# Gathers of the value rows two places further ahead in GpSimd's order, in a hybrid decoder step with product-key experts

## What is computed

```python
act = jax.nn.gelu(jnp.einsum('thkd,td->thk', u_emb[idx], tb).astype(jnp.float32))
return jnp.einsum('thk,thkd->td', (g * act).astype(tb.dtype), v_emb[idx])
```

## Time and profile before

| | us |
|---|---|
| three runs | 2326.48, 2330.93, 2336.44; median 2330.93 |
| the profiled execution, its own time | 2352.97 |
| its span, first to last instruction | 2351.2 |
| busy in the span | TensorE matmul 1711.3 (73%), VectorE 1556.3 (66%), ScalarE 540.0 (23%), GpSimd 918.6 (39%) |
| DMA moved in the span | 798.79 MB, mean 340 GB/s |

### The profile page before, as it was taken

One profiled execution on the slowest core, in us unless ns is written; L12 is line 12 of the kernel. 1 busy time (PEld: TensorE's weight loads), 2 busy tenths in 40 slices (PEclk: granted clock), 3 DMA queues, 4 the chain that ended last, 5 costly groups with the idle time before them and its releaser, 6 DMA issues.

```text
span 2351.2 us, 30749 instructions
## 1 busy us (share of the span) xinstructions
PE 1711.3 (73%) x10511; PEld 1183.2 (50%) x10511; DVE 1556.3 (66%) x4092; ACT 540.0 (23%) x1574; POOL 918.6 (39%) x840
## 2 busy tenths in 40 slices
PE   7999977687898898987899879996534434343433
PEld 7899976443587776765577667663100000000000
DVE  4634178777578547888756776435388878877855
ACT  4446255100135123432122341111001000010000
POOL 0000001156434454543454455555644454444442
PEclk8999999757799999997899999997655566566566
DMA  6487767289999999986799899987999999999995
GB/s 226 148 269 251 249 198 266 81 307 405 398 398 381 402 409 359 359 312 215 275 379 349 337 388 388 401 336 289 397 421 422 421 417 421 417 415 413 414 421 234
DMA packets 181932, 798.79 MB, mean 340 GB/s; under 512 B 20977, under 2 KB 21233, under 8 KB 147857
## 3 DMA queue, kind: packets, MB, share of 16 engines
q0 software_dynamic: 119808, 570.48, 61.7%
q1 hardware_dynamic: 59616, 219.40, 25.6%
q10 hardware_dynamic: 2352, 6.95, 1.0%
HBM read 779.88 MB, written 12.14 MB: 337 GB/s over the span
## 4 chain that ended last, share of the span: by engine, by line
PE 20%; DMA 14%; DVE 11%; issue 5%; POOL 3%; ACT 0%; another core or an unknown queue 0%; POOLq 0%; DVEq 0%; ACTq 0%; SPq 0%
PE ps L490 11%; DMA s_exr<-in_uv,s_gidx 6%; DMA s_wr<-in_uv,s_gidx 3%; PE ps L817 3%; DVE s_exr L1722 2%; PE ps L800 2%; PE ps L473 2%; DMA s_scr<-in_uv,s_gidx 2%; DMA s_hnr<-in_uv,s_gidx 1%; DMA s_exr<-in_v,s_gidxT 1%; POOL s_exr L1379 1%; DVE s_wr L1722 1%; DVE s_scr L1722 1%; PE ps L839 0%; POOL s_exr L1365 0%
## 5 line engine op out<-in xcount | busy, mean ns | idle before, releaser
L490 PE MATMUL ps<-s_hnr,s_wr 128*128 128x256 f32 (+2 forms) x3968 | 679.9, 330 | 48.5 <-ACT s_hist_p L978 24.5
L490 PEld LDWEIGHTS ps<-s_hnr,s_wr 128*128 128x128 f32 x3968 | 610.3, 197 | 128.0 <-issue 73.8
L1334 POOL DMA_INDIRECT s_exr<-in_u,s_gidx x288 | 310.2, 1077 | 838.3 <-DVE s_act_z L1722 449.3
L1722 DVE CUSTOM_DVE_ANT_0 s_exr<-s_exr,s_tbg 128x1024 f32<-128x1024 f32 x407 | 491.7, 1221 | 167.1 <-DMA s_exr<-in_u,s_gidx 100.1
L1346 POOL DMA_INDIRECT s_exr<-in_v,s_gidxT x256 | 279.4, 1091 | 197.8 <-issue 89.8
L817 PE MATMUL ps<-s_exr,s_sw 128*32 128x512 f32 x476 | 156.5, 1044 | 164.0 <-DVE s_sw L1751 164.0
L1379 POOL DMA_INDIRECT s_exr<-in_uv,s_gidx x119 | 140.3, 1179 | 149.2 <-PE ps L817 120.9
L800 PE MATMUL ps<-s_exr,s_zb 128*32 128x512 f32 x1072 | 152.7, 659 | 41.6 <-DMA s_exr<-in_v,s_gidxT 29.6
L1427 DVE SCALAR_TENSOR_TENSOR s_scr<-s_scr,s_par 128x128 f32<-128x128 f32 (+2 forms) x288 | 122.2, 426 | 50.3 <-ACT s_scr L984 41.5
L817 PEld LDWEIGHTS ps<-s_exr,s_sw 128*32 128x32 f32 x476 | 25.0, 157 | 244.0 <-DVE s_sw L1751 191.6
L1157 ACT ACTIVATE s_gth<-s_g 128x4 f32<-128x4 f32 x64 | 13.1, 205 | 566.3 <-DVE s_g L1740 566.3
(11 more groups left out here) (314 smaller groups left out, 2695.6 us busy)
## 6 DMA issues: line engine op xcount, KB each, us to landing
s_wr<-in_wstream SPq DMA_DIRECT2D x360, 512.0 KB
s_tbg<-s_h2e ACTq DMA_DIRECT2D x36, 128.0 KB
s_exr<-in_u,s_gidx POOLq DMA_INDIRECT x288
s_exr<-in_v,s_gidxT POOLq DMA_INDIRECT x268
s_xr<-in_sample_h_in SPq DMA_DIRECT2D x8, 512.0 KB, 7.9
s_scr<-in_sample_h_in SPq DMA_DIRECT2D x8, 512.0 KB, 7.3
out_sample_h_out<-s_xr SPq DMA_DIRECT2D x8, 512.0 KB
out_sample_h_out<-s_scr SPq DMA_DIRECT2D x8, 512.0 KB
```

Of the source, the lines that this page charges most:

```text
L490: last = pe.matmul(ps[:, o % 2, 0:n], wring[:, slot, k, :], rhs[:, k, :], start=k == 0, stop=k == KT - 1)
L1334: pool.indirect_dma_start(uring[n % URING], None, a["u"], bass.IndirectOffsetOnAxis(ap=gidx[:, i % 2, s:s + 1], axis=0)).then_inc(u_in[n % ...
L1722: dve.tensor_tensor_reduce(out=u, in0=u, in1=tbg[:, i % 2, :], scale=1.0, scalar=0.0, op0=ALU.mult, op1=ALU.add, accum_out=act_z[:, i % 2, ...
```

## The change

Only the order in which GpSimd issues its gathers changes, for groups 0 to 7 of v with groups 1 to 8 of u. At the start of each pass two row sets of v are issued; from then on row set t + 2 of v stands ahead of u slot t, where row set t stood. The last two u slots of a pass follow each other with no v between them. No gather is added or removed, no buffer and no wait changes its form.

```diff
             for i in range(WIDE - 1):
+                gather_v(i, 0)
+                gather_v(i, 1)
                 for t in range(GT):
-                    gather_v(i, t)
+                    if t + 2 < GT:
+                        gather_v(i, t + 2)
                     gather_u(i + 1, t)
             for t in range(GT):
                 gather_old(WIDE - 1, t)
```

## The result

The changed kernel takes 2375.59 us in the median of five runs (2370.29 to 2378.06) against 2330.93 us of the kernel before, here also five runs: a ratio of 1.0185, 95% interval 1.0167 to 1.0203. The change makes the kernel slower by 44.7 us, where 17.5 us were forecast. The direction and the mechanism of the loss were right. The size was missed by a factor of 2.55, and the gain that the sum counted on did not come.

The account below looks back on a forecast made before the run. TensorE and the arrival of rows were taken to come near to setting the pace. Loss 33.5 us (15 + 3 + 4 + 9 + 2.5) less gain 16 made + 17.5 us: 2348 us, range given 2314 to 2376, the forecast's own 2343 to 2376.

Parts of the forecast that it names:

- the gain: TensorE's waits for v rows: 16 us saved, mainly 11.4 at the 1410 us stall and 3.5 near 1307; ends 0 and 22.
- The coupling (step 1): u slot 4k - 2, not 4k, stands behind the v gather waiting for TensorE's quad; VectorE gets two u slots later.
- The decode stage: 500 to 625 us: late u rows delay VectorE, then TensorE; three payments of 4.8 us, 15 us lost, ends 0 and 29.
- The bracket: Landing time of a gather, between 6.74 us for the quickest on the chain and 17.3 us in the decode stage's crowd.
- 785 to 910: DMA engines full, VectorE's next norm waits for the dots before it; two places at 2.1 us each, 3 us lost.
- 910 to 1150: 910 to 1040: 3 us, partly hidden behind TensorE; 1040 to 1150: late u slot 2 delays the dot before L612, 4 us.
- 625 to 785, 1150 to 1325: Same pattern of late u rows, half or more hidden behind TensorE's dense work; 2 us lost.
- The end of the alternation: Slots 26 and 27 stand behind the v gather of 1619.10, so the first `gather_old` goes late; 2.5 us, with longer landing 8.
- (B): Rival, a wash: lateness half hidden, or the 1410 stall's gain lost at the next DMA wait; 2332 us, chance 0.28.
- (A): Rival, relief wins: u's 4.8 us paid once inside VectorE's idle time, TensorE's stalls go; 2315 us, chance 0.17.
- (C): Rival: late dots delay TensorE, its quad v, v u, in every quad, landing as in the crowd; + 66, 2397 us, chance 0.08.

Follow-up runs that it names:

- pass 0 alone: Changed gather order in the first of the eight passes only (decode stage), other seven as in the kernel before; ratio 1.0071.
- the second profile: Later profile of the unchanged kernel before, made beside the experiments in a job of 2334 us; span 2330.1 us.
- pass12: Changed gather order in passes 1 and 2 only (623 to 920 us), the others as in the kernel before; ratio 1.0036.
- pass56: Changed gather order in passes 5 and 6 only (1227 to 1497 us), the others as in the kernel before; ratio 0.9983.

## Why the prediction was right in direction and wrong in size

**The coupling (step 1) is shown.** It rests on the run that kept the waiting gather's place, on TensorE's quads in two places under both orders, on the steps from one to three places, and on the traces: GpSimd's queue runs empty before each blocked v gather of the decode stage, and rows land no later than before. What failed is the size of three terms of the loss, and the gain, which is the largest error.

**The decode stage, 15 us forecast: 17 to 25.** The run of pass 0 alone costs 17 us, the trace of the whole change shows 24.7 in that stage by VectorE's first dots and 17.8 by TensorE's quads (from quad 0 to quad 0 of the next group, -2.8 to 15.0 us of difference). The prediction had one payment of 4.8 us if the queue never runs empty and six if each quad lets it run empty, and took three, naming no reason. The failed step is this choice: the queue ran empty, or nearly so (14% at the first), at each of the six. From quad 0 to quad 6 the difference grows by 23.4 us, in steps of 5.3, 7.2, 1.6, 4.3, 0.4 and 4.5, so four quads pay 4.3 to 7.2 us and two hardly any. Slot 6's row took 535.85 - 525.88 = 10.0 us to land though nothing but one v gather had been issued for 17 us before it, and why isn't shown; SyncE's queue had a share of 18% from 526 to 530 us and of 49% from 530 to 534. The bracket's lower end, 6.74 us, wasn't the quickest either: 4.1 and 4.2 us stand in the traces.

**785 to 910, 3 us forecast: 10.** Here the step failed that took the loss as two places paid once. From slot 0 to slot 3 of group 3 the difference of the dots grows from 20.2 to 25.7 us, VectorE waiting some 3 us a row where it didn't wait; slot 15 adds 2.7 more, and the norm at the end of the stage stands behind both, 29.2 us late. The waits of about 4 us behind slot 15 were there before. VectorE at slots 3 and 15, after, then in the second profile of before:

```profile
841.43 1.23 DVE L1725 CUSTOM_DVE_ANT_0 s_exr<-s_exr,s_tbg 128x1024 f32<-128x1024 f32 x1 [2.88 <-DMA s_exr<-in_u,s_gidx]
...
896.21 1.23 DVE L1725 CUSTOM_DVE_ANT_0 s_exr<-s_exr,s_tbg 128x1024 f32<-128x1024 f32 x1 [7.09 <-DMA s_exr<-in_u,s_gidx]
```

```profile
815.73 1.22 DVE L1722 CUSTOM_DVE_ANT_0 s_exr<-s_exr,s_tbg 128x1024 f32<-128x1024 f32 x1
...
866.82 1.23 DVE L1722 CUSTOM_DVE_ANT_0 s_exr<-s_exr,s_tbg 128x1024 f32<-128x1024 f32 x1 [4.35 <-DMA s_exr<-in_u,s_gidx]
```

pass12, which holds this stage, costs 8 us.

**910 to 1150, 3 + 4 us forecast: 12.** The first dots of groups 4 and 6 differ by 30.2 and 42.1 us, and TensorE's first quads after them by 30.2 and 36.9, so about 7 us are TensorE's and the rest is VectorE's lag at group 6. Around it went as worked out: VectorE's dot waits 4.17 us for its row where it did not wait, and TensorE's L612 stands 8.27 us behind it, 4.14 in the earlier trace rows.

```profile
1137.40 1.23 DVE L1725 CUSTOM_DVE_ANT_0 s_exr<-s_exr,s_tbg 128x1024 f32<-128x1024 f32 x1 [4.17 <-DMA s_exr<-in_u,s_gidx]
```

**The small terms.** 625 to 785: 2 us forecast, 0 seen by the first dots, which had shown the whole 24.7 by then, and 5.0 by the quads, which had shown 17.8. 1150 to 1325: 2 forecast, none of it seen at TensorE (its quads keep a difference of 36.9 us from quad 2 of group 4 to quad 2 of group 5). The end of the alternation: 2.5 us forecast, 2.5 seen (37.3 us at the last quads, 39.8 at group 9). `gather_old` follows 14.3 us after the blocked v gather, where it was 11.3:

```profile
1638.90 0.94 POOL L1346 DMA_INDIRECT s_exr<-in_v,s_gidxT  x1 [5.03 <-PE ps L800]
...
1653.23 1.65 POOL L1365 DMA_INDIRECT s_wr<-in_v,s_gidxT  x1 [0.30 <-issue]
```

**The gain, 16 us forecast: none in the whole change.** Both stalls shrank. The one of 4.74 us (5.07 in the second profile) is now 2.67, and that of 10.46 us in the second profile (9.9 in the earlier trace rows), which was to go, is 3.14. TensorE at the former, after, then around the latter, after and then in the second profile of before:

```profile
1340.78 1.92 PE L800 MATMUL ps<-s_exr,s_zb 128*32 128x512 f32 x16 [2.67 <-DMA s_exr<-in_v,s_gidxT]
```

```profile
1431.36 3.64 PE L800 MATMUL ps<-s_exr,s_zb 128*32 128x512 f32 x16 [6.03 <-DVE s_zb L1767]
...
1440.17 1.92 PE L800 MATMUL ps<-s_exr,s_zb 128*32 128x512 f32 x16 [3.14 <-DMA s_exr<-in_v,s_gidxT]
...
1452.99 1.22 PE L490 MATMUL ps<-s_scr,s_wr 128*128 128x256 f32 x2 [4.22 <-DVE s_scr L1653]
```

```profile
1395.14 1.92 PE L800 MATMUL ps<-s_exr,s_zb 128*32 128x512 f32 x16 [2.05 <-DVE s_zb L1764]
...
1409.43 3.22 PE L800 MATMUL ps<-s_exr,s_zb 128*32 128x512 f32 x16 [10.46 <-DMA s_exr<-in_v,s_gidxT]
```

But TensorE now stands 6.03 us for s_zb, the weights of the quad, instead of 2.05, and 4.22 us for a product of VectorE (L1653) where it did not stand: together 8.2 us paid for 7.3 saved. The granted clock falls in both new stalls: it is 0.50 in the quad at 1431.36, which runs 3.64 us instead of 1.92, and 0.59 in the products from 1454.00 to 1460.10. By the quads' differences TensorE goes from 36.9 us late before the stall near 1307 to 32.2 behind it, 4.7 won where 3.5 were forecast, and is back at 36.9 by quad 2 of group 6. VectorE never won anything there: at s_zb it is 36.2 us late (1431.11 against 1394.89), with 3.5 us of waits for u rows at slots 0 and 1 of group 7 against 2.7 before. At L1653 it is 38.2 us late, so some 2 of the 4.22 us are late u rows and the rest is TensorE having run ahead of it. This is the step that failed: the prediction took a stall of TensorE as saved in full, and did not ask where TensorE next waits for VectorE, which that stall doesn't delay. It also had no term for late u rows between 1325 and 1500 us, and no reason for leaving it out. The 2.05 us for s_zb just ahead of the largest stall (2.04 in the first profile, at 1396.91) already showed that VectorE is the one that ends last there. The rival that had the gain given back, (B), named DMA and not VectorE.

pass56, the two passes with the gain alone, gives -4 us where -15 were in the sum, and its 0.9983 is no further from 1 than the unchanged kernel's 0.9971. Its trace shows the same giving back: the quads stand 3.9 us ahead of the second profile before the stall near 1307, 5.4 behind it, and 2.2 at quad 2 of group 6, again after 5.94 us for s_zb. So a gain of 4 us is not shown even there.

**The sum.** By TensorE's quads: 17.8 us in the decode stage, 5.0 from there to group 2, 10.2 to group 3, 6.8 to quad 2 of group 4, 0.3 from there to group 7 and 2.5 at the end, 42.6 in all; by timing 44.7. So the loss is some 43 to 45 us instead of 33.5 and the gain about nothing instead of 16, and the missing gain is the larger share of the 27 us. The time, 2375.59, lies 0.4 us inside the forecast's own range, 2343 to 2376, and the range was wide enough for errors of this size. That the profiled execution (2371.6) lies near 2352.97 + 17.5 = 2370.5 bears nothing out: the first profile of the kernel before is one as the 2350 us jobs give it.

**The rivals.** (A), relief, fell: v's waits did shrink, but VectorE's wait for u grew by 134 us. (B) had a gain given back, which came, but by VectorE; and it had the lateness half hidden, which it was not. (C) had the loop right that late dots delay TensorE and TensorE delays v, and the wrong size: median landing times of 6.6 to 12.9 us by stage for a u row, not 17. With three places the kernel goes beyond (C)'s 66 us, 1.0487 or 114 us.

**The rule of the skill.** The Trainium skill ("DMA: Bandwidth & Descriptors", Anatomy of one DMA) gives 2.0 us plus bytes at 436 GB/s, by that page 3.2 us for such a gather, an estimate. The trace doesn't agree: the quickest gather found in it landed in 4.1 us, the median u row of the decode stage in 8.7, and behind a blocked v gather slot 6 took 10.0 us and slot 10 559.80 - 553.55 = 6.25 us. By that rule the loss of the decode stage would nearly have vanished; the measurement decides.

## What to carry to other kernels

When one engine issues gathers for two consumers, look at which gather in its order waits for whom: what matters is how many buffers of the other stream are still in flight when that wait opens, against the landing time. Here a slot lasts some 4.5 us in the decode stage (144.6 us for 32), and a row lands in 9 to 12 us in the median. With one place of lead two slots are in flight beyond TensorE's place, with two one, with three none. An estimate from these numbers: two slots about cover a landing and one doesn't, and the runs agree, with nothing that can be told for the first place and 1.6 to 1.9% for the second. A stall that an edit removes is a gain only as far as the next wait for an engine that the edit doesn't speed up; find that wait before the stall is counted.

## What was not expected of the hardware

A gather issued into a nearly empty GpSimd queue still took 6.25 and 10.0 us to land for 512 KB while SyncE's queue was busy (93.2% of the DMA engines' time from 549 to 551.5 us, ahead of the former, and 18 to 49% during the latter). And holding gathers back made the single one quicker, 11.8 to 8.7 us in the median of the decode stage, while the kernel became slower. The same kernel took 2328 us in one job and 2350 in another, a difference as large as half the change, with the ratio of the change the same in both; a trace of the one sort against one of the other showed less than half of the loss.
